# Dealing attention's ticks two at a time between the steps of an expert gather

## The reference

```python
p = jax.nn.softmax(jnp.where(mask, s, -jnp.inf), axis=-1)          # attention: an exponential
...
u = jnp.take(expert_u, it, axis=0)                                   # PEER: 128 rows for each token
a = jax.nn.gelu(jnp.einsum('tkd,td->tk', u, ht), approximate=False) * gt
vv = jnp.take(expert_v, it, axis=0)
return jnp.einsum('tk,tkd->td', a.astype(vv.dtype), vv)
```

## Time and profile before

| | us |
|---|---|
| median of 3 runs | 3324.57 (3320.59 to 3329.91) |
| the profiled execution, its own time | 3332.64 |
| its span, first to last instruction | 3330.7 |
| PE busy | 2658.0 (80% of the span) |
| DVE busy | 2424.1 (73%) |
| ACT busy | 1185.6 (36%) |
| POOL busy | 1233.4 (37%) |
| mean granted TensorE clock | 0.904 |
| moved by DMA | 1247 MB, mean 374 GB/s |

### The profile page before, as it was taken

The page is one execution under the profiler, slowest core; times in us unless marked ns, Lnnn a source line. Parts: engine busy times, 40 slices in busy tenths (PEclk is TensorE's granted clock), DMA queues, the critical chain, the costliest instruction groups (busy, mean ns, idle before and its releaser), DMA issues. The chain is left out here.

```text
span 3330.7 us, 29036 instructions
## 1 busy us (share of the span) xinstructions
PE 2658.0 (80%) x8188; PEld 1476.4 (44%) x8188; DVE 2424.1 (73%) x5581; ACT 1185.6 (36%) x3370; POOL 1233.4 (37%) x1085
## 2 busy tenths in 40 slices
PE   5798788768868888788768888788868899777776
PEld 4575544334445443365445444365445444322322
DVE  7775788788877788756976888746967878754544
ACT  1141233358822333313822333314842223323222
POOL 0110245344444445333334444434333345433332
PEclk9899899988788999888778999988768999999999
DMA  8782799999999999999999999999999999999997
GB/s 320 271 288 92 276 420 409 364 360 346 351 381 414 384 421 412 418 386 369 377 374 418 395 421 414 413 376 366 375 357 379 412 402 412 417 422 404 421 421 324
DMA packets 266714, 1247.23 MB, mean 374 GB/s; under 512 B 20117, under 2 KB 106533, under 8 KB 135351
## 3 DMA queue, kind: packets, MB, share of 16 engines
q0 software_dynamic: 156064, 1106.97, 82.2%
q1 hardware_dynamic: 110482, 138.36, 11.6%
q10 hardware_dynamic: 8, 0.06, 0.0%
HBM read 1243.18 MB, written 7.36 MB: 375 GB/s over the span
## 5 line engine op out<-in xcount | busy, mean ns | idle before, releaser
L1554 PE MATMUL psum<-space 128*128 128x512 f32 x3192 | 1618.2, 646 | 411.3 <-ACT space L1598 365.6
L1688 POOL DMA_INDIRECT space<-in_peer_uv,expert x1024 | 1200.6, 1172 | 1833.2 <-PE psum L1554 1170.3
L1629 DVE CUSTOM_DVE_ANT_0 space<-space,h 128x1024 f32<-128x1024 f32 x1024 | 1246.6, 1222 | 655.3 <-DMA space<-in_peer_uv,expert 630.2
L1554 PEld LDWEIGHTS psum<-space 128*128 128x128 f32 x3192 | 618.3, 203 | 1166.0 <-issue 573.9
L1587 ACT ACTIVATE space<-space 128x2 f32<-128x2 f32 x512 | 103.9, 203 | 1492.8 <-DVE space L1629 1482.3
L713 PE MATMUL psum<-space 128*128 128x256 f32 (+2 forms) x1584 | 388.0, 403 | 69.8 <-DMA space<-in_w_in_c 33.1
L713 PEld LDWEIGHTS psum<-space 128*128 128x128 f32 x1584 | 315.2, 202 | 161.2 <-issue 55.0
L1598 ACT ACTIVATE space<-ident,space 128x128 f32<-128x128 f32 x798 | 278.1, 387 | 1.7 <-PE psum L1554 0.2
L1231 PE MATMUL psum<-space 128*128 128x256 f32 x1024 | 263.1, 386 | 13.8 <-DVEq L574 5.3
L1231 PEld LDWEIGHTS psum<-space 128*128 128x128 f32 x1024 | 198.7, 195 | 139.5 <-issue 105.5
L1590 ACT ACTIVATE space<-space,gate 128x1 f32<-128x1 f32 x1024 | 245.6, 287 | 16.8
(11 more groups left out here) (181 smaller groups left out, 1821.9 us busy)
## 6 DMA issues: line engine op xcount, KB each, us to landing
space<-in_peer_w_q SPq DMA_DIRECT2D x32, 1024.0 KB
space<-in_ada_w SPq DMA_DIRECT2D x12, 2048.0 KB, 15.7
space<-in_ada_w POOLq DMA_DIRECT2D x24, 1024.0 KB, 5.6
space<-in_w_in_c SPq DMA_DIRECT2D x24, 1024.0 KB
space<-in_peer_uv,expert POOLq DMA_INDIRECT x1024
space<-in_w_out_ab SPq DMA_DIRECT2D x8, 1024.0 KB
space<-skewed SPq DMA_DIRECT2D x32, 256.0 KB
space<-in_w_out_c SPq DMA_DIRECT2D x8, 1024.0 KB
```

What stands on the lines that cost most here:

```text
L1554: last = nc.tensor.matmul(b.bank[part][:, :], b.diag2[:, n % DIAGS, :], b.pairs[:, p % PAIRS, 1, part * BANK:(part + 1) * BANK], start=(p ...
L1629: dve.tensor_tensor_reduce(out=row, in0=row, in1=b.h[:, tile(q), :], scale=1.0, scalar=0.0, op0=ALU.mult, op1=ALU.add, accum_out=b.dots2[: ...
L1688: pool.indirect_dma_start(out=b.pair_rows[q % PAIRS], out_offset=None, in_=ins["peer_uv"], in_offset=bass.IndirectOffsetOnAxis(ap=b.expert ...
```

## The change

After the ticks of a phase have been spread over its picks, each entry of `done` that lies within attention's ticks is rounded down to an even number of attention ticks. So attention's ticks are no longer dealt singly: two always follow each other after the same pick, and the picks between get none. Neither the work nor its order within one engine's attention program changes; what changes is how attention's instructions and those of the picks are interleaved on PE, ACT and DVE. SP's and POOL's programs don't read `done`.

```diff
     def __init__(self, n_picks):
-        self.done, self.total, self.n_picks = [], 0, n_picks
+        self.done, self.total, self.n_picks, self.paired = [], 0, n_picks, (0, 0)
+
+    def pairs(self, first, last):
+        self.paired = (self.total + first, self.total + last)
 ...
         self.done += [self.total + int(np.sum(ends <= i + 1 + 1e-6)) for i in range(end - first)]
+        lo, hi = self.paired
+        for i in range(first, end):
+            if lo <= self.done[i] < hi:
+                self.done[i] -= (self.done[i] - lo) % 2
         at = [self.total + mark for mark in marks]
 ...
             attended = next((i for i, part in enumerate(body) if part.attends), 0)
+            plan.pairs(ticks_in(body[:attended]), ticks_in(body[:attended + 1]))
             middle, end = plan.spread(costs_of(body) + following[:chosen], first, until, ticks_in(body[:attended]),
                                       ticks_in(body))
```

## The result

The changed kernel takes 3381.06 us in the median of 4 runs (3374.14 to 3390.64), the kernel before 3327.24 in 4 runs beside it. The ratio is 1.0165 with a 95% interval of 1.0126 to 1.0203: some 54 us slower. The forecast was 3316.4 with a range of 3300 to 3345, so the time lies outside it on the slow side.

What follows compares the result with a forecast made beforehand. DVE was taken as nearest to a bound in the attention stages, its idle time the gain: A -4.7, C -7.3, B +3.8, together -8.2 us, from 3332.6 to 3324.4 profiled, 3316.4 as median; range 3300 to 3345.

Steps and rivals of the forecast that it cites:

- DVE's idle time in A, B and C: Three attention stages (picks 110 to 191, 402 to 439, 649 to 706): DVE nearest to a bound, busy 88%, 83%, 84%.
- the gathers would take up what PE gives back: Rival: in A and C waits for gathers grow as PE's shrink; no gain, B costs 3.8, 3328 us; chance 0.16.
- named as free: 11 pairs in A and 8 in C whose diagonal is ready early, so nothing new is exposed.
- named as exposed: 14 pairs in A, 9 in C: PE's owed sum precedes the next pair, its GELU follows this one; 0.62 us each.
- B's +3.8: Stage B: 13 new pairs holding exponentials at 0.29 us each, no loads saved; 3.8 us slower.
- the bound of +11.2: Upper bound for B: 0.86 us for each of 13 pairs, instead of 3.8.
- Rival 3: PE falls to its lower clock in A and C; exposed pairs cost 2.0 us each, +23.5, 3348 us; chance 0.23.
- the ring: Exposed pair's loop from ACT's last copy to the next: 7.5 us upper clock, 10.3 lower, against 8.3 without stall.
- a mean clock: Exposed pairs in A and C: clock 0.79 read as 42% of the time at PE's lower level.
- the biases: SP's loads in the stages: handled at nothing, hidden, their progress depending on the same semaphores as before.
- The middle that was no middle: Cost of an exposed pair in A and C: 0.62 us, taken between 0.4 and 0.84.
- 26.3 us of holds: DVE's waits ended by PE, for scores or products with V: 13.4 us in A, 12.9 in C, counted as gain.

Runs made afterwards that it cites:

- residue2_filled: residue2 with two 128x256 products of identity and zeros on PE ahead of each sum in the attention stages; 3357.6 us (1.0102).
- The fillers: Two 128x256 products of identity and zeros on PE ahead of each attention-stage sum, added to the changed kernel (3351.5 us) and to residue2 (3357.6 us).
- residue2: The changed kernel with the first and third attention stages' pairs always after picks that leave 2 when divided by 3; 3438.2 us (1.0351).
- before_tanh: The kernel before with Tanh in place of GELU, so no table switches in the attention stages; 3318.4 us (0.9968).

## Why the prediction was wrong

**What it had right.** The bound (DVE's idle time in A, B and C, nothing outside), who ends it (PE, and ACT through PE), the count of loads (60 and 99), in part which sums are caught, and that the gathers would take up what PE gives back. None of the pairs at picks 151 to 169, named as free, was held by a late score, and 10 of A's 14 named as exposed were; but those at 135, 141, 147, 681 and 687, named as free, were held as well. B's +3.8 against +8.1, inside the bound of +11.2, is luck: it was priced by holds, which didn't grow there. Rival 3, a loss through PE's lower clock level, is the nearest to what happened, but not by its own signs: the holds are above its 30 us in A and C together (49.3 + 20.9), the clock is 0.72 and 0.75 where it wanted 0.70 or less, and by its price of 2.0 us for a pair such a clock would have brought no measurable loss (it wanted 0.65 for that).

**The step that failed: the ring.** The prediction let the loop of an exposed pair run from the scores through L1053 and the exponential to a copy by ACT: 7.5 us at the upper level, 10.3 at the lower. The copy that holds the GELU is that of the second tick, and it waits for PE's transposes of the first tick, its products with V, the second scores and the second transposes. These were left out of the sum, though the text said that PE's second tick stands ahead of the next sum. In the trace above they are 0.55 + 1.00 + 1.12 + 0.66 = 3.3 us in place of L1053 and the exponential, 1.57 together. The ring is 10.4 us with only the sum at the lower level, and 13.8 with all of it, against the 8.3 of DVE and gathers. With a sum of 1.98 as in the earlier trace rows it would be 10.4 - 1.5 = 8.9, and residue2_filled shows 8.8 to 8.9. So a pair with a caught sum costs some 0.6 us at the upper level, not nothing, 2.1 with the sum alone at the lower, and 5.5 with all of it, not 2.0.

**The second step: a mean clock.** The share at the lower level was taken from the stage's clock, 0.79, as 42%. But the sum comes right behind PE's wait for the diagonal, and there it takes 3.78, 3.46 and 3.78 us in the three cases shown (the earlier trace rows and the two timelines above). It is not always so: the 1.98 us of the earlier trace rows stand behind a wait of 1.03. Over all of A, the sums behind a wait of 1 us or more take 3.3 us in the mean, 8 of them in the kernel before and 16 in the changed one; the share of 42% gives 0.58 x 1.98 + 0.42 x 3.78 = 2.7. A mean over a stage does not tell the clock where the chain runs. The fillers price this: 30 us in the changed kernel, 80 in residue2.

**A term put at nothing: the biases.** SP's loads were taken as hidden, since each stage has them. In pairs DVE asks for two biases at once, and the kernel has two buffers for them (`bias2`, L1052). DVE's waits for the bias and for the gate together rose from 7.7 to 14.2 us in B and from 7.3 to 10.3 in C, some 9.5 us of the loss. That the two buffers are the reason is argued from the code; no run shows it.

**The middle that was no middle.** Between 0.4 and 0.84 us for an exposed pair I took 0.62. DVE's holds grew by 34.3 us in A; laid on its 14 exposed pairs, that is 2.5 each, though the prediction had them shrink by 13.4 first. The bounds were both made from a ring too short and a clock too high, so the middle between them was worth nothing.

**The gain.** 26.3 us of holds were put down as if all could be had. before_tanh shows 11 us when every load is gone, because the waits for gathers grow. How much of the 11 a quarter of the loads would have brought, no run shows. (A slip of no weight: the earlier trace rows give 0.28 us for a pair in B, not 0.29.)

**Two rules weighed beforehand.** The rule on the clock gate (the Trainium skill, "TensorE: Matmul & The Clock Gate", Part 1), that the clock follows how busy the array lately was, spoke against the change, and the runs agree: 0.72 where PE pauses in the ring, 0.88 with 96 instructions more. The rule on the switch of tables (the Trainium skill, "ScalarE: Activation LUTs", "What ACT_TABLE_LOAD costs"), 2.66 us with a drain, is not what this trace shows: ACT's copy ends at 2391.38, at 2391.40 the load starts, and the GELU starts 1.29 us later.

## What to carry to other kernels

Saving work on an engine that isn't the bound is worth only the waits that it ends; before a new order is made for its sake, write out the whole ring that runs through each engine's queue, in the order of the queue, up to the instruction that repeats, and compare it with the bound's work for the same stretch. Where one engine's step has to be caught between two bundles of another's, the place of the bundle can be worth more than its size: here 96 us between two residues of the same pairs. And price a step on TensorE by rows of such steps behind such waits (3.3 us here), not by the mean clock of its stage (2.7).

## What the hardware showed that I had not expected

Products that compute nothing made the kernel faster. Two of 128x256 ahead of each sum took the changed kernel from 3381 to 3351 us and residue2 from 3438 to 3358; PE was busy 17 us less in A (218.5 to 201.5) with 96 instructions more, at a clock of 0.88 for 0.72. And the same order of A took 277.7 us in one execution, with a clock as low as 0.56 for 52 us, and 256.9 in another. A ring that feeds itself would do that, a lower clock making it longer and the longer ring making PE's waits longer; the traces fit this, but no run was made to show which comes first.
